# Narrow f32 products of a three-block transformer kernel as four partial sums in four column groups

## What is computed

```python
# first block, layer 0: z = h @ ab_w_in, whose columns hold, among the wide parts,
#   16 columns of the low-rank gate:  log_a comes from (h @ w[:, 1024:1040]) @ gla_gate_up   (16 -> 256)
#    8 columns of index weights:      iw = h @ w[:, 3664:3672]
rel = relu(einsum('bqhd,bsd->bqhs', iqb, ik))
score = einsum('bqhs,bqh->bqs', rel, iwb) * idx_scale        # the top keys of score are kept
# second block: mLSTM gates, 8 columns of m_w_in_2: 4 input gates and 4 forget gates
i_gate, f_gate = h @ m_w_in_2[:, 3072:3076], h @ m_w_in_2[:, 3076:3080]
```

## Time and profile before

| | |
|---|---|
| device time, 3 runs | 3436.68, 3441.87, 3441.95 us; median 3441.87 |
| span of the profiled execution (first to last instruction) | 3435.1 us |
| PE busy | 3336.9 us, 97% of the span |
| DVE, ACT, POOL busy | 2003.6, 1111.1, 134.1 us |
| DMA | 361.20 MB, mean 105 GB/s |
| mean granted TensorE clock | 0.989 |

### The profile page before, as it was taken

The page is one execution under the profiler, slowest core; times in us unless marked ns, Lnnn a source line. Parts: engine busy times, 40 slices in busy tenths (PEclk is TensorE's granted clock), DMA queues, the critical chain, the costliest instruction groups (busy, mean ns, idle before and its releaser), DMA issues. The chain is left out here.

```text
span 3435.1 us, 38647 instructions
## 1 busy us (share of the span) xinstructions
PE 3336.9 (97%) x13840; PEld 2509.0 (73%) x13840; DVE 2003.6 (58%) x2815; ACT 1111.1 (32%) x1503; POOL 134.1 (4%) x230
## 2 busy tenths in 40 slices
PE   6999899998999999999999999999999999999999
PEld 3446788886678888667888854588887757888887
DVE  6684666535668864565766359766644464455523
ACT  2223422223632222444433210343333343242222
POOL 1000000000000000000000040000000100000000
PEclk9999999999999999999999999999999999999999
DMA  7222355542125543212223311122233222222222
GB/s 287 80 70 80 131 181 192 176 133 74 49 86 199 192 147 104 68 44 80 94 95 95 96 58 56 51 86 98 96 95 129 79 74 74 98 92 86 97 98 86
DMA packets 100426, 361.20 MB, mean 105 GB/s; under 512 B 11152, under 2 KB 11168, under 8 KB 100064
## 3 DMA queue, kind: packets, MB, share of 16 engines
q1 hardware_dynamic: 79088, 280.34, 24.6%
q0 software_dynamic: 20080, 75.27, 6.6%
q10 hardware_dynamic: 1152, 4.19, 0.3%
HBM read 357.66 MB, written 2.10 MB: 105 GB/s over the span
## 5 line engine op out<-in xcount | busy, mean ns | idle before, releaser
L2393 DVE TENSOR_TENSOR weight_lo<-weight_ring,weight_hi 128x1024 fp32r<-128x1024 f32 (+1 forms) x458 | 552.9, 1208 | 899.2 <-ACT weight_hi L1654 893.3
L1654 ACT ACTIVATE weight_hi<-weight_ring 128x1024 fp32r<-128x1024 f32 (+1 forms) x458 | 478.7, 1046 | 1558.8 <-PE proj_banks L919 972.3
L919 PE MATMUL proj_banks<-h_lo,weight_hi 128*128 128x512 f32 x1672 | 650.5, 389 | 0.0
L919 PE MATMUL proj_banks<-h_hi,weight_hi 128*128 128x512 f32 x1312 | 510.5, 389 | 0.5 <-DVE weight_lo L2393 0.5
L919 PE MATMUL proj_banks<-h_hi,weight_lo 128*128 128x512 f32 x1312 | 510.4, 389 | 0.0
L919 PEld LDWEIGHTS proj_banks<-h_lo,weight_hi 128*128 128x128 f32 x1672 | 313.8, 188 | 64.9
L919 PEld LDWEIGHTS proj_banks<-h_hi,weight_hi 128*128 128x128 f32 x1312 | 246.3, 188 | 52.3 <-issue 0.8
L919 PEld LDWEIGHTS proj_banks<-h_hi,weight_lo 128*128 128x128 f32 x1312 | 246.3, 188 | 51.0
L919 PE MATMUL proj_banks<-mid_lo,weight_hi 128*128 128x512 f32 x704 | 273.9, 389 | 0.0
L919 PE MATMUL proj_banks<-mid_hi,weight_lo 128*128 128x512 f32 x704 | 273.9, 389 | 0.0
L919 PE MATMUL proj_banks<-mid_hi,weight_hi 128*128 128x512 f32 x704 | 273.9, 389 | 0.0
(11 more groups left out here) (426 smaller groups left out, 5200.2 us busy)
## 6 DMA issues: line engine op xcount, KB each, us to landing
weight_ring<-in_w_up SPq DMA_DIRECT2D x176, 512.0 KB, 3.3
ada_ring<-in_ada POOLq DMA_DIRECT2D x96, 512.0 KB, 3.8
weight_ring<-in_w_dn SPq DMA_DIRECT2D x64, 512.0 KB, 3.5
weight_ring<-in_w_br SPq DMA_DIRECT2D x32, 512.0 KB, 3.2
weight_ring<-in_w_upr SPq DMA_DIRECT2D x32, 512.0 KB, 3.2
weight_ring<-in_w_dnr SPq DMA_DIRECT2D x32, 512.0 KB, 3.2
weight_ring<-in_w_dn SPq DMA_DIRECT2D x32, 384.0 KB, 3.1
cond<-in_ada POOLq DMA_DIRECT2D x20, 512.0 KB, 4.6
```

What stands on the lines that cost most here:

```text
L919: last = mm(proj.banks[:, u % RING, :], stationary(home + n)[:, w], moving(k), start=k + m == 0, stop=k == kt - 1 and m == 2)
L1654: return nc.scalar.activation(out, in_, func, **kw)
L2393: return v.tensor_tensor(out, a, b, op)
```

## The change

The low-rank gate and index weights become one product over all 32 columns of `small_weights`: for each k the result goes to the 32 output partitions of column group k mod 4, so that k = 0 to 3 start four groups and k = 4 to 7 are added to them (`quarter_sums`). The bank then holds four partial sums, each of 32 columns. ACT copies all 128 partitions to T(53). The low-rank gate's next product takes them as they are: `gate_up` is stored four times, at 32-row steps, with zeros in rows 16 to 31 of each, so that it adds the quarters too. The index weights come from four small products with the constant `sum_iw`, which picks rows 16 to 23 of each quarter and adds them; all four go to one bank, and ACT copies them at once. The mLSTM gates are made the same way: `quarter_sums(("mg", 0))` ahead of tile `mqk` 7, a copy to T(57), and one product each for `mi` and `mf` with `sum_m`.

```diff
-            keys += [("iw", t) for t in range(NB)] + [("glow", 0)]
+            keys += [("glow", 0), ("iw", 0)]
         if name == "mqk":
-            keys += [("mi", 0), ("mf", 0)]
+            keys = keys[:-1] + [("mg", 0), ("mqk", 7), ("mi", 0), ("mf", 0)]
...
-        self.gate_up = sb("gate_up", [16, 256])
+        self.gate_up = sb("gate_up", [P, 256])
...
+    def quarter_sums(key):
+
+        bank = open_bank(proj, key)
+        for k in range(KD):
+            q = slice(32 * (k % 4), 32 * (k % 4) + 32)
+            last = mm(bank[q, :], c.wsmall[:, 32 * k:32 * k + 32], H(k), start=k < 4, stop=k >= 4, skip_group_check=True)
+        last.then_inc(proj.full_sem, 1)
...
-            for n in range(NB):
-                bank = open_bank(proj, ("iw", n))
-                for k in range(KD):
-                    last = mm(bank[:, 0:8], h_tok(k, n), c.wsmall[:, 32 * k + 16:32 * k + 24], start=k == 0, stop=k == 7)
-                last.then_inc(proj.full_sem, 1)
-            bank = open_bank(proj, ("glow", 0))
-            for k in range(KD):
-                last = mm(bank[0:16, :], c.wsmall[:, 32 * k:32 * k + 16], H(k), start=k == 0, stop=k == 7)
-            last.then_inc(proj.full_sem, 1)
+            quarter_sums(("glow", 0))
...
+    bank = open_bank(proj, ("iw", 0))
+    pe.wait_ge(*proj.emptied(("glow", 0)))
+    for n in range(NB):
+        last = mm(bank[:, 8 * n:8 * n + 8], T(53)[:, n * P:(n + 1) * P], c.const("sum_iw"), start=True, stop=True)
+    last.then_inc(proj.full_sem, 1)
     pe.wait_ge(s["iq_ready"], 5)
...
-    pe.wait_ge(*proj.emptied(("glow", 0)))
     for t in range(2):
-        mm(open_bank(mix, ("gate", t)), c.gate_up[0:16, t * P:(t + 1) * P], T(53)[0:16, :], start=True, stop=True) \
+        mm(open_bank(mix, ("gate", t)), c.gate_up[:, t * P:(t + 1) * P], T(53), start=True, stop=True) \
...
     for t in range(3, 8):
+        if t == 7:
+            quarter_sums(("mg", 0))
         split_feature_tile("mqk", t, c.H_hi, m_lo)
+    pe.wait_ge(*proj.emptied(("mg", 0)))
     for n, key in enumerate((("mi", 0), ("mf", 0))):
-        bank = open_bank(proj, key)
-        for k in range(KD):
-            last = mm(bank[0:4, :], c.wsmall[:, 32 * k + 24 + 4 * n:32 * k + 28 + 4 * n], H(k), start=k == 0, stop=k == 7)
-        last.then_inc(proj.full_sem, 1)
+        mm(open_bank(proj, key)[0:4, :], c.const("sum_m")[:, 4 * n:4 * n + 4], T(57), start=True, stop=True).then_inc(proj.full_sem, 1)
...
-    for n in range(NB):
-        copy_out(proj, ("iw", n), c.small[:, 8 + 8 * n:16 + 8 * n], n=8, scale=(8 ** -0.5) * (64 ** -0.5))
-    copy_out(proj, ("glow", 0), T(53)[0:16, :], rows=16)
+    copy_out(proj, ("glow", 0), T(53))
+    copy_out(proj, ("iw", 0), c.small[:, 8:40], n=32, scale=(8 ** -0.5) * (64 ** -0.5))
...
     for t in range(9):
+        if t == 7:
+            copy_out(proj, ("mg", 0), T(57))
```

More of the change, by code:

```diff
@@ L107, in other_constants @@
         "pick_wide": np.tile(np.eye(4, 32).reshape(1, 128), (P, 1)),
+        "sum_iw": np.tile(np.eye(32)[:, 16:24], (4, 1)),
+        "sum_m": np.tile(np.eye(32)[:, 24:32], (4, 1)),
     }
@@ L2583, in vector_program @@
         if b == 1:
-            dve.wait_ge(*proj.emptied(("iw", 3)))
+            dve.wait_ge(*proj.emptied(("iw", 0)))
         for h in range(8):
@@ L3470, in lay_out @@
     out["positions"] = f["positions"][0]
-    out["gla_gate_up"] = f["gla_gate_up"][0]
+    out["gla_gate_up"] = np.zeros((4, 32, 256), np.float32)
+    out["gla_gate_up"][:, 0:16] = f["gla_gate_up"][0]
+    out["gla_gate_up"] = out["gla_gate_up"].reshape(P, 256)
     out["m_bias"] = np.ascontiguousarray(f["m_b_gates_2"][0].reshape(2, 4).T)
```

## The result

The change makes the kernel slower. Median 3448.82 us (8 runs, 3445.73 to 3459.37) against 3438.51 us (8 runs, 3433.24 to 3442.62) of the kernel before; ratio 1.0034, 95% interval 1.0022 to 1.0046, so 12 us (8 to 16) longer. I had forecast 3423 us, 0.55% less.

The account below looks back on a forecast made before the run. PE was taken as the bound, busy nearly throughout. Savings of 11.7 and 7.4 us, together 19.1, took the 3435.1 us span to 3416.0; 6.8 us for the median of runs gave 3422.8, say 3423 us, range 3414 to 3431.

Parts of the forecast that it names:

- place A: Index weights and low-rank gate, ahead of the fifth rotation and the index products: 11.7 us saved.
- five rivals: Column groups take turns 0.18; part of the gain comes back later 0.09; nothing measurable 0.04; slower 0.02; better than forecast 0.05.
- The slower rival: Clock stays low through the index stage, costing 30.6 us instead of 2.0: 9.5 us slower, 3451; chance 0.02.
- column groups, 16 passes: The quarters' passes at both places run four groups at a time: 1.9 us, or 6.9 if one at a time.
- earlier start of the rotation: DVE starts its fifth rotation at 88.07 instead of 102.14, 14.0 us earlier.
- wait ahead of the index products: PE waits some 4.6 us for DVE's rotation, from 85.7 to 90.3.
- low clock behind it: After PE's wait the clock runs at 0.50 into the index stage: 2.0 us charged, bounds 0 and 3.3.
- loading of larger constants: At the start, 120 KB more of constants at 354 GB/s: 0.3 us charged in full.
- second tile of `mv` waits for the taps: PE waits 1.6 us for the bank that DVE's three taps on tile 7 must end with.
- wait for the q = 2 chunk: PE, through with q = 0 and 1 of `mv`, waits 1.0 us for the next chunk.
- place B: mLSTM gates between `mqk` tile 7 and `mv`: 13.8 us removed, less added passes and waits, 7.4 us saved.
- the low bound: 16 passes of the quarters take 1.7 us with four column groups at a time.

Follow-up runs that it names:

- e1: The kernel before with an unused tensor of 16 floats per partition behind `others`, moving later tensors 64 bytes: 3471.5 us, ratio 1.0091.
- e4: The changed kernel with its two selecting constants in a tensor of their own behind all others: 3418.7 us, ratio 0.9941 to the kernel before.
- e9: e4 with the mLSTM gates as in the kernel before: 3422.6 us, ratio 0.9948 to the kernel before.
- e12: e4 with two of the three modulation rows ahead of DVE's fifth rotation moved behind it: 3415.6 us, ratio 0.9927 to the kernel before.
- e10: e4 with index weights and low-rank gate as in the kernel before: 3430.6 us, ratio 0.9975 to the kernel before.
- e11: e4 with column group k // 2 instead of k mod 4: 3417.9 us, ratio 0.9934 to the kernel before.
- e7: The kernel before with an unused tensor of 64 floats per partition behind `others`, moving activations 256 bytes: 3439.9 us, ratio 0.9999.

## Why the prediction was wrong

**The step that failed** stands under place A: "Start: `gate_up` grows from 16 to 128 KB and `others` by 8 KB." I charged the bytes (0.3 us), and nothing for the place of what lies behind them, though I wrote of place A's gain that I "find nothing behind it that is tied to an earlier moment". The missing term is +31 us by e1 (25 to 37), and the change against e4 gives 0.93% by the ratios (1.0034 and 0.9941), 32 us: more than all that the change gains. None of the five rivals had it. Only the last of my signs of being wrong did, that the span might change elsewhere by more than 3 us. The slower rival was another mechanism: a clock that stays low through the index stage, which the profile refutes (1.00 again from 94.3 to 129 us).

A second, smaller error is in the base: I added 6.8 us to the span, the distance of the median of three executions. The eight of the result have their median only 3.4 us above it. With that, my 19.1 us would have given 3419 us, and e4 came out at 3418.7.

**The rest, term by term**, with e4 as the change without that shift:

| term | predicted us | measured us |
|---|---|---|
| column groups, 16 passes | 1.9 (1.7 to 6.9) | 1.92, start to next start 1.86 |
| earlier start of the rotation | 14.0 | 14.1 in the change |
| wait ahead of the index products | 4.6 | 4.54 |
| low clock behind it | -2.0 | half of 4.08 = -2.0 |
| loading of larger constants | -0.3 | quarters start at 81.86 in the change as before, at 82.10 in e4, 82.53 in e9, 82.71 in e12: 0 to -0.9 |
| place A | 11.7 | 11.7 (e9, waits), 12.1 (e4, wait near 810), 18 (13 to 23) by the ratio of e9 |
| second tile of `mv` waits for the taps | 1.6 | 1.43 |
| wait for the q = 2 chunk | 1.0 | 0.60 (0.77 in e4) |
| place B | 7.4 | 7.0 (e4 against e9, by spans), 6.9 (e10, waits), 9 (6 to 11) by the ratio of e10 |
| both | 19.1 | 18.7 by spans, 20 (14 to 26) by the ratio |

That e9's waits give place A the very 11.7 that I forecast is in part luck: its quarters started 0.7 us later than before, where I had charged 0.3, and in e4 the same place brings 12.1.

For place B by its own rows: from the end of tile 7 to the transposes it was 35.86 us before, and in e4 it is 26.76 us and 1.86 for the quarters, 7.2 less:

```profile
1397.48 1.92 PE L1049 MATMUL proj_banks<-h_tiles,small_weights 128*32 128x512 f32 x16
...
1405.05 1.88 PE L1367 MATMUL proj_banks<-scratch,sums 128*4 128x512 f32 x4
...
1409.95 0.50 PE L965 MATMUL proj_banks<-weight_hi,h_hi 128*128 128x512 f32 x1 [1.45 <-DVE scratch L2416]
...
1431.81 0.41 PE L1372 MATMUL mix_banks<-squares,scratch 4*128 4x4 f32 x4
```

**The column groups.** The rule from the Trainium skill, "TensorE: Matmul & The Clock Gate", Part 3, that a weight load overlaps matmuls in flight only where row groups differ, would have made this 6.9 us. The trace does not agree: 16 passes that share all 128 rows took 1.92. My argument for the low bound (only two passes of a group follow each other) was not the reason either, by e11. Why L1167 reached only 1.4 at a time, with eight passes in a row in each group, was not tried.

**What stays open** is the mechanism behind the distance. The runs show that it is relative, that shifts of 256 and 512 bytes are free, that it depends on the form (at +64, `h_hi,weight_lo` loses nothing) and that in e1 it reaches products whose own operands did not move against each other: those of `late_rounded` with `weight_hi` take 394 ns between 3120 and 3200 us, where the kernel before has 389. (They alternate with products of the moved `h_lo`.) A pass of `late_rounded,weight_lo` with `late_rounded,weight_hi` behind it has both operands and the next weights where they were, and yet the next start comes 232.4 ns behind its own in e1, 226.0 before. So a clash of a pass's own streaming reads with the next weight load, which would fit the dependence on the distance, is not enough by itself. No run takes the mechanism apart, nor asks whether reads and writes of other engines take part.

## What to carry to other kernels

A constant added in the middle of an SBUF layout moves every tensor behind it. Put new small tensors last (e4), or pad them to 256 bytes per partition (a shift by 256 was free in e7), and compare the addresses of the large matmul operands before and after, as one compares the order of instructions. When a gain that is visible at its place has melted by the end, follow a few waits that both traces share, and count passes in an equal dense window: it tells a slower pass from a new wait in two rows. Here a price of about 1% on every pass (31 us) outweighed two tuned places (20 us).

## What the runs showed of the hardware

- One-pass products of 128x512 came every 226 ns on average when the weights and the activations lay as in the kernel before (multiples of 512 bytes apart) or 256 or 512 bytes from that, 228.5 at +64, 232.0 at +128, 232.9 at -64. At +64 a form lost between 0 (`h_hi,weight_lo`, 226.5 ns) and 3% (the passes at the end of the kernel that stream `weight_hi` against a stationary `relu_hi` or `relu_lo`, 233.4 ns); at +128 and -64 all three forms of L919 lost (232.4 and 233.3 ns). The Trainium skill, "TensorE: Matmul & The Clock Gate", Part 2 (Step-by-step), says that loading the next tile's weights doesn't steal read bandwidth from the running matmul, as PE has a read port for each. By that alone one would expect no dependence on the distance. These runs show one, and leave open whether those two reads are its cause.
- Four column groups of 32 columns ran side by side: the 16 passes of 8 f32 products, 512 columns streamed in each, took 1.9 us, 3.7 at a time by the 0.43 us of one pass, in either order of the groups, and across them in another order than the program's (e11).
